# Linear attention in a hybrid decoder step: the output formed with tokens on partitions

## Chip, cores and metric

The kernel runs on one core of one Trainium2 chip. The metric is the device time of one execution in microseconds (us), lower is better. Engines are called as in the profile: PE (TensorE, matmuls), PEld (its weight loads), DVE (VectorE), ACT (ScalarE), POOL (GpSimd) and SP (the engine that issues most DMAs). In a matmul one operand is *stationary* (loaded into the array) and the other is *moving* (streamed through it); all tensors here are float32, and each float32 matmul shows as two records in the trace.

## What is computed

One layer of a decoder trunk for 512 prompt tokens and 8 single-token samples, width 1024. The layer has a modulated layer norm, one large projection, a recurrent branch A, a gated linear attention branch B, a merge of both, and a mixture of experts. The change touches branch B only:

```python
# per head h of 4 (dk=128, dv=256), in chunks of 64 tokens; S: state of 128x256
attn  = where(tri, q_in @ k_in.T, 0)             # 64x64 per chunk and head
o     = attn @ v + q_in @ S_start                # 64x256 per chunk and head
S     = S * decay + k_out.T @ v
# samples, one token each, with a state of their own:
S_s   = S_s * exp(la) + outer(k, v);   o_s = q @ S_s
# both:
o     = o * rsqrt(mean(o**2) + 1e-6) * gla_norm_g   # mean over the 256 values of a head
y_b   = o * silu(gate)
```

## The kernel before, in words

Activations lie with features on the 128 partitions and the 520 tokens (512 + 8) along the free dimension: `hT`, `G` (the gate after silu), `O` (branch B's output), `Q` (q and k), `A` and `Z` are all 8 x 520 per partition. The kernel is written with explicit semaphores, one instruction stream for each engine. PE's work is a fixed list of jobs (`plan_jobs`, L81): job number n writes PSUM banks 2*(n%3) and the next one, so there is a ring of three slots; `start` (L1459) waits until the job three earlier was freed by its reader, `done` counts a job, and other engines wait for that count (`await_job`). Bank 6 holds scores, bank 7 the attention output.

Weights come as 2 MB tiles through a ring; SP issues each load (L466) once PE has reported an older tile as used. Column tiles of `w_in`, `p_a` and `p_b` are used by `project` (L1486), 16 matmuls of 128x128 by 260 columns for one job (helper line L1482).

The stage in question is the chunk loop (PE L1610, DVE L1167, ACT L910), 8 chunks and at the same time 8 samples. For chunk n PE does in this order:

1. scores of 4 heads, 64 columns each (L1616), into bank 6;
2. the state's increment `ds`, 4 matmuls of 256 columns (L1621);
3. half 0 of the gate projection `gg` (L1628, helper L1482);
4. the output, features on partitions: for each of 8 (head, half) pairs one matmul with the values stationary and the masked scores moving (L1636, 64 columns) and, from chunk 1 on, one with the state stationary and q moving (L1639);
5. half 1 of `gg` (L1641), then a wait for DVE's sample state (L1644);
6. the sample's output `os`: 8 matmuls with its state stationary and one moving column (L1647).

DVE masks the scores (L1176, L1178), updates `S` from `ds` (L1187, L1189), decays the sample's state (L1196) and adds the outer product (L1199), then reports `st_ready`. SP then loads the next sample's values broadcast to all partitions (L507), stores the finished state (L514) and loads the one after the next (L494). ACT applies silu to `gg` (L906), copies `os` (L913) and the output out of bank 7 into `O` (L916).

After the loop the norm is made for all tokens at once, beside the projection `ga`: ACT squares a head (L922), PE sums over the features with a matmul of ones (`squares`, L1656, job `ss`, 4 matmuls of 260 columns for one of 4 heads), DVE scales (L1205), ACT takes the root (L926), DVE the reciprocal (L1211) and two multiplies (L1213), then the gating (L1217). Then follow `pa`, `ga`, `pa`, `gb`, `pb`, `gb`, `pb` in groups of four jobs, the output projection `wo`, routing and the experts.

ACT keeps one table of functions; a change of function set shows as ACT_TABLE_LOAD.

Of the kernel before, what the change touches and what calls it, by code (L numbers as in the profile page):

```python
# [27 lines left out]
P = 128  # L28
D = 1024
# [51 lines left out]
def plan_jobs():  # L81
# [21 lines left out]
    for n in range(NCH):  # L103
        jobs += [("ds", n), ("gg", n), ("os", n)]
    for c in range(4):
        jobs += [("ga", c), ("ss", c)]
    jobs += [("pa", c) for c in range(4)]
# [43 lines left out]
def build(nc, t, outs):  # L151
# [6 lines left out]
    with ExitStack() as ctx:  # L158
# [49 lines left out]
        attm = [area(TB + 2048 + 256 * j, HEADS, CH) for j in range(2)]  # L208
        sq = [area(TB + 1040 * j, 2, NT) for j in range(2)]
        rms = [area(TB + 2080 + NT * j, NT) for j in range(2)]  # L210
        bc = area(A0, 4, D)
# [52 lines left out]
        scan_mask = area(2 * WT + 3080, NT)  # L264
        v_samp = area(2 * WT, D)
        v_samp = keep(D)

        rt = [TB]
# [109 lines left out]
        st_out = [sem(f"st_out{j}") for j in range(2)]  # L378
        sq_ready = sem("sq_ready")
        var_ready = sem("var_ready")  # L380
        rms_ready = sem("rms_ready")
        mod_out = sem("mod_out")
        mod_back = sem("mod_back")
# [225 lines left out]
        def _(pool):  # L609
# [34 lines left out]
            link(pool.memset(scan_mask[:, 0:T:CH], 0.0))  # L644
            link(pool.memset(scan_mask[:, T:NT], 0.0))
            pool.sem_inc(consts, 1)

# [95 lines left out]
        def _(sc):  # L743
# [160 lines left out]
            def gate(c):  # L904
                await_job(sc, ("gg", c))
                sc.activation(halves(G[:, c, :]), two_halves(("gg", c)), ACT.Silu, bias=fp[:, c, R_BIN + 4:R_BIN + 5])\  # L906
                  .then_inc(freed(("gg", c)), 1)

            sc.wait_ge(mod_out, 16)
            for n in range(NCH):  # L910
                gate(n)
                await_job(sc, ("os", n))
                sc.activation(O[:, :, T + n:T + n + 1], slot_banks(("os", n))[:, 0, 0:8].unsqueeze(2), ACT.Copy)\  # L913
                  .then_inc(freed(("os", n)), 1)
                sc.wait_ge(o_done, n + 1)
                sc.activation(O[:, :, n * CH:(n + 1) * CH], ps[:, 7, :].rearrange("p (a b) -> p a b", b=CH), ACT.Copy)\  # L916
                  .then_inc(o_copied, 1)

            def square(h):
                if h >= 2:  # L920
                    await_job(sc, ("ss", h - 2))
                sc.activation(sq[h % 2], O[:, 2 * h:2 * h + 2, :], ACT.Square).then_inc(sq_ready, 1)  # L922

            def root(h):
                sc.wait_ge(var_ready, h + 1)
                sc.activation(rms[h % 2], rms[h % 2], ACT.Sqrt).then_inc(rms_ready, 1)  # L926

# [7 lines left out]

            sc.wait_ge(o_copied, NCH)
            sc.wait_ge(freed(("os", 7)), INDEX[("os", 7)] // 3 + 1)
            for j in range(2):
                sc.wait_ge(st_out[j], 16 * (NS // 2))
            square(0)  # L940
            sc.wait_ge(s_out, 32)
            merge_gate("ga", 0)
            square(1)
            for h in range(3):
                root(h)
                merge_gate("ga", h + 1)
                if h < 2:
                    square(h + 2)
            root(3)
            for c in range(4, 8):  # L950
                merge_gate("ga", c)
# [78 lines left out]
        def _(v):  # L1030
# [116 lines left out]
            def copy_vt(c):  # L1147
# [16 lines left out]
            for c in range(2, 8):  # L1164
                copy_vt(c)

            for n in range(NCH):  # L1167
                q = 64 * (n % 2)
# [3 lines left out]
                if n == 0:  # L1172
                    v.wait_ge(kt_ready, 1)

                am = attm[n % 2][q:q + 64]
# [27 lines left out]
            def variance(h):  # L1203
                await_job(v, ("ss", h))
                link(v.tensor_scalar(halves(rms[h % 2]), two_halves(("ss", h)), 1.0 / DVH, RMS_EPS, ALU.mult, ALU.add))  # L1205
                v.sem_inc(freed(("ss", h)), 1)
                v.sem_inc(var_ready, 1)

            def rescale(h):
                v.wait_ge(rms_ready, h + 1)  # L1210
                link(v.reciprocal(rms[h % 2][:], rms[h % 2][:]))  # L1211
                for d in range(2):
                    link(v.scalar_tensor_tensor(O[:, 2 * h + d, :], O[:, 2 * h + d, :], fp[:, 4 + d, R_MISC:R_MISC + 1],  # L1213
                                                rms[h % 2][:], ALU.mult, ALU.mult))

            def gate(c):
# [3 lines left out]
            v.wait_ge(freed(("gg", 7)), INDEX[("gg", 7)] // 3 + 1)  # L1220
            variance(0)
            variance(1)
            for h in range(HEADS):
                rescale(h)
                if h + 2 < HEADS:
                    variance(h + 2)
                gate(2 * h)
                gate(2 * h + 1)

# [228 lines left out]
        def _(pe):  # L1458
# [149 lines left out]
            pe.wait_ge(kt_ready, 1)  # L1608

            for n in range(NCH):  # L1610
                q, tile = 64 * (n % 2), n // 2
# [39 lines left out]
            def squares(h):  # L1651
                pe.wait_ge(sq_ready, h + 1)
                out = start(("ss", h))
                for half in range(2):
                    for d in range(2):
                        ins = pe.matmul(out[:, half, 0:HALF], ones[:], sq[h % 2][:, d, half * HALF:(half + 1) * HALF],  # L1656
                                        start=(d == 0), stop=(d == 1))
# [189 lines left out]
```

## Time and profile before

| | us |
|---|---|
| median of 3 runs | 1518.23 |
| lowest, highest run | 1515.2, 1527.52 |
| span of the profiled execution | 1523.0 |
| PE busy in it | 1262.4 |
| DVE, ACT, POOL busy | 413.6, 307.3, 127.0 |

The span of the profiled execution is the only time given of it; the three other runs were not profiled. Times in the trace count from the span's start. `PEclk` is the mean clock that the chip granted TensorE, as a share of the full 2.4 GHz; it has two levels, 1.2 and 2.4 GHz, so a mean of 0.75 is half the stretch at either. "[0.68 <-DVEq L1201]" means: the engine was idle for 0.68 us before this instruction and what ended that was DVE's queue at line 1201. "x16" counts records, two for a float32 matmul.

### The profile page before, as it was taken

To read this page: it belongs to the slowest core of one execution; us is meant where nothing else is said; L and a number is where in the kernel's file an instruction comes from. 1 tells how busy PE (TensorE), PEld (TensorE's weight loads), DVE (VectorE), ACT (ScalarE), POOL (GpSimd) and SP (SyncE) were. 2 spreads that over 40 slices of the span, in tenths; PEclk is the share of its full clock that TensorE was granted. 3 is DMA by queue.
4 is the path that set the end of the run, shared out by engine and by line. 5 is a ranking of instruction groups with operands and counts; after the bars stand their busy time and mean duration, and the time that the engine had idled before them with its cause. 6 is when DMAs were issued, how large, how long until landed. Compare 5 with 4: busy or idle time off the path is not lost.

```text
span 1523.0 us, 18481 instructions
## 1 busy us (share of the span) xinstructions
PE 1262.4 (83%) x6402; PEld 815.4 (54%) x6403; DVE 413.6 (27%) x704; ACT 307.3 (20%) x433; POOL 127.0 (8%) x203
## 2 busy tenths in 40 slices
PE   3899999999999999999987379798887977788710
PEld 3687878787878888888643223233332332233300
DVE  3326240423332260010386601111111111111156
ACT  3255550410000320000100012121211111111221
POOL 0100000000000000000000111111111111111134
PEclk9899999998878999999998579999998999889965
DMA  8744412124232213413003457996999999999631
GB/s 286 238 171 157 176 56 69 48 72 151 83 110 70 84 56 114 165 56 111 31 15 155 193 194 299 389 348 262 396 397 379 393 367 394 383 378 391 259 119 55
DMA packets 69930, 307.24 MB, mean 202 GB/s; under 512 B 10039, under 2 KB 18744, under 8 KB 56917
## 3 DMA queue, kind: packets, MB, share of 16 engines
q1 hardware_dynamic: 59786, 294.77, 50.5%
q0 software_dynamic: 6272, 10.14, 2.1%
q10 hardware_dynamic: 3820, 1.60, 0.4%
q8 instruction: 38, 0.62, 0.2%
q14 instruction: 14, 0.11, 0.0%
HBM read 298.35 MB, written 18.55 MB: 208 GB/s over the span
## 4 chain that ended last, share of the span: by engine, by line
PE 64%; DMA 18%; DVE 8%; issue 4%; ACT 3%; SPq 2%; ACTq 0%; POOL 0%; POOLq 0%; DVEq 0%; PEldq 0%
PE ps L1482 33%; DMA mem<-in_we_up 13%; PE ps L1750 12%; PE ps L1759 5%; PE ps L1709 3%; DMA mem<-in_w_mod 2%; PE ps L1639 2%; PE ps L1742 2%; PE ps L1636 1%; PE ps L1621 1%; DVE mem L1445 1%; PE ps L1647 1%; DMA mem<-in_we_gate 1%; DVE mem L1444 1%; PE ps L1515 1%
## 5 line engine op out<-in xcount | busy, mean ns | idle before, releaser
L1482 PE MATMUL ps<-mem 128*128 128x260 f32 (+1 forms) x2336 | 546.6, 396 | 10.3 <-ACT mem L813 3.9
L1482 PEld LDWEIGHTS ps<-mem 128*128 128x128 f32 (+1 forms) x2336 | 454.5, 196 | 95.3 <-issue 12.6
L1750 PE MATMUL ps<-mem 128*64 128x512 f32 x1120 | 286.7, 671 | 99.9 <-DMA mem<-in_we_up 78.4
L1750 PEld LDWEIGHTS ps<-mem 128*64 128x64 f32 x1120 | 89.7, 154 | 270.9 <-issue 270.9
L1424 DVE TENSOR_TENSOR mem<-mem,ps 64x512 f32<-64x512 f32 x35 | 24.1, 690 | 431.3 <-ACT mem L1002 431.3
L1759 PE MATMUL ps<-mem 128*64 128x512 f32 x560 | 129.2, 604 | 3.4 <-issue 3.4
L1002 ACT ACT_TABLE_LOAD x35 | 44.9, 1283 | 372.5 <-PE ps L1750 372.5
L1759 PEld LDWEIGHTS ps<-mem 128*64 128x64 f32 x560 | 37.5, 138 | 66.8 <-issue 64.5
L710 POOL DMA_INDIRECT pair_scratch<-mem x35 | 32.7, 934 | 458.2 <-DVE mem L1416 458.2
L1416 DVE COPY mem<-ps 64x512 f32<-64x512 f32 x70 | 48.1, 688 | 78.1 <-PE ps L1759 77.0
L1709 PE MATMUL ps<-mem 128*128 128x512 f32 x128 | 59.8, 628 | 0.0
L1742 PEld LDWEIGHTS ps<-mem 64*128 64x128 f32 x288 | 34.4, 200 | 32.6 <-issue 32.6
L931 ACT ACTIVATE mem<-ps,mem 128x520 f32<-128x520 f32 x16 | 11.1, 694 | 169.9 <-PE ps L1482 169.8
L1742 PE MATMUL ps<-mem 64*128 64x64 f32 x288 | 39.4, 278 | 4.0 <-DMA mem<-hf_scratch,mem 4.0
L651 POOL IOTA mem<- 128x4 int32 x1 | 0.1, 137 | 510.0 <-DVEq L1218 510.0
L1709 PEld LDWEIGHTS ps<-mem 128*128 128x128 f32 x128 | 25.4, 201 | 31.7 <-issue 31.6
L688 POOL DMA_INDIRECT mem<-hf_scratch,mem x37 | 35.9, 970 | 31.5 <-POOL mem L719 29.7
L1814 PEld LDWEIGHTS ps<-mem 64*128 64x128 f32 x140 | 19.4, 210 | 29.5 <-issue 29.5
L1238 DVE TENSOR_TENSOR mem<-mem,ps 128x520 f32<-128x520 f32 x8 | 5.6, 696 | 102.9 <-PE ps L1482 102.9
L906 ACT ACTIVATE mem<-ps,mem 128x520 f32<-128x520 f32 x8 | 5.6, 694 | 133.8 <-PE ps L1482 133.8
L1009 ACT ACTIVATE mem<-ps 128x256 f32<-128x256 f32 x35 | 13.5, 384 | 94.0 <-PE ps L1814 94.0
L1515 PE MATMUL ps<-mem 128*9 128x128 f32 x768 | 25.9, 292 | 5.2 <-DMA mem<-in_w_mod 5.2
(284 smaller groups left out, 988.7 us busy)
## 6 DMA issues: line engine op xcount, KB each, us to landing
mem<-in_we_gate SPq DMA_DIRECT2D x32, 2048.0 KB, 12.0
mem<-in_we_up SPq DMA_DIRECT2D x32, 2048.0 KB, 16.5
mem<-in_we_down SPq DMA_DIRECT2D x32, 2048.0 KB, 8.9
mem<-in_w_in SPq DMA_DIRECT2D x14, 2048.0 KB, 8.5
mem<-in_w_mod SPq DMA_DIRECT2D x12, 2048.0 KB, 12.0
out<-mem SPq DMA_DIRECT2D x13, 512.0 KB, 5.3
mem<-in_state_gla SPq DMA_DIRECT2D x8, 512.0 KB, 3.9
mem<-v_scratch SPq DMA_DIRECT2D x8, 512.0 KB, 4.3
```

Source lines behind the costliest of these rows:

```text
L688: pool.indirect_dma_start(xg[j][0:CAP, :], None, hf_dram, bass.IndirectOffsetOnAxis(ap=gidx[j][0:CAP, 0:1], axis=0), bounds_check=NT - 1, ...
L710: pool.indirect_dma_start(pair_dram, bass.IndirectOffsetOnAxis(ap=sidx[j][0:CAP, 0:1], axis=0), yb[j][0:CAP, :], None, bounds_check=PAIRS ...
L1002: sc.activation(sg[j][CAP:2 * CAP, :], ps[0:CAP, 2 + j, :], ACT.Silu).then_inc(sg_ready[j], 1)
L1416: v.tensor_copy(yb[j][0:CAP, q * 512:(q + 1) * 512], ps[CAP * q:CAP * q + CAP, 4 + j, :])\
L1424: v.tensor_tensor(act[j][0:CAP, :], sg[j][CAP:2 * CAP, :], ps[CAP:2 * CAP, 2 + j, :], ALU.mult)\
L1482: ins = pe.matmul(out[0:m, h, 0:HALF], w[:, k, col:col + m], src[:, k, h * HALF:(h + 1) * HALF], start=(k == 0), stop=(k == KD - 1))
L1515: pe.matmul(o, cs[:, k, :], w[:, k, g * P:(g + 1) * P], start=(k == 0), stop=False)
L1639: ins = pe.matmul(o, S[n % 2][:, h, d * P:(d + 1) * P], Q[:, h, cols], start=False, stop=True)
L1709: ins = pe.matmul(out[0:r, h, :], Z[:, k, i * P:i * P + r], wo[h][:, k, :], start=(k == 0), stop=(k == KD - 1))
L1742: ins = pe.transpose(ps[:, j, k * CAP:(k + 1) * CAP], xg[j][0:CAP, :].rearrange("s (p k) -> s k p", k=KD)[:, k, :], ident[0:CAP, 0:CAP])
L1750: ins = pe.matmul(ps[CAP * q:CAP * q + CAP, 2 + j, :], xT[j][:, k, :], ring[3 * slot + q][:, k, :], start=(k == 0), stop=(k == KD - 1))
L1759: ins = pe.matmul(ps[CAP * q:CAP * q + CAP, 4 + j, :], acT[j][:, k, :], wd[:, k, q * 512:(q + 1) * 512], start=(k == 0), stop=(k == 3))
```

## The change

Step 4 is turned round. The masked scores of a head are now stationary (64 columns) and that head's 256 values move; for the second term q is stationary and the state moves. Two heads lie side by side: head 2a writes PSUM partitions 0 to 63, head 2a+1 partitions 64 to 127. The scores tile is padded with zero rows to 128. The output now has tokens on partitions, so the mean over a head's features is along the free dimension, and ACT forms it for each chunk (square with a running sum, root, with DVE's reciprocal between, two scaled copies into `osb`). Four PE transposes of 128x128 for each chunk, put into the `os` job of the next chunk, turn it back, and ACT writes them into `O`. The sample's output is formed with a masked q stationary (32 columns for each head, four heads side by side) and the state moving; DVE sums it over samples, and it is normed once. The `ss` jobs, the long norm and their buffers are gone; two small jobs, `oT` and `sT`, take the last transposes.

```diff
-    for c in range(4):
-        jobs += [("ga", c), ("ss", c)]
+    jobs += [("ga", 0), ("oT", 0), ("ga", 1), ("sT", 0), ("ga", 2), ("ga", 3)]
...
+            link(pool.memset(qm[:], 0.0))
+            link(pool.affine_select(out=qm[:], in_=qm[:], compare_op=ALU.not_equal, fill=1.0, base=0,
+                                    pattern=[[0, HEADS], [1, NS], [-1, 32]], channel_multiplier=0))
...
+            def mean_squares(o, junk, k):
+                link(sc.activation(junk, o, ACT.Square, scale=DVH ** -0.5, accum_out=o_ms[:, k // 2, k % 2:k % 2 + 1]))
+            def heads_of(n):
+                sc.wait_ge(o_done, n + 1)
...
+                for a in range(2):
+                    mean_squares(o[:, a, :], osb[n % 2][:, a, :], 2 * n + a)
+                sc.activation(o_rs[:, n, :], o_ms[:, n, :], ACT.Sqrt, bias=rms_eps[:, 0:1]).then_inc(root_ready, 1)
+                sc.wait_ge(rms_ready, n + 1)
+                for a in range(2):
+                    ins = sc.activation(osb[n % 2][:, a, :], o[:, a, :], ACT.Copy, scale=o_rs[:, n, a:a + 1])
...
+            def fill_heads(n, src):
+                for d in range(2):
+                    for hh in range(2):
...
+                        ins = sc.activation(dst, src[:, (2 * hh + d) * P:(2 * hh + d + 1) * P].rearrange("p (a i) -> p a i", a=2),
+                                            ACT.Copy, scale=fp[:, 4 + d, R_MISC:R_MISC + 1])
...
             for n in range(NCH):
+                heads_of(n)
                 gate(n)
                 await_job(sc, ("os", n))
-                sc.activation(O[:, :, T + n:T + n + 1], slot_banks(("os", n))[:, 0, 0:8].unsqueeze(2), ACT.Copy)\
-                  .then_inc(freed(("os", n)), 1)
-                sc.wait_ge(o_done, n + 1)
-                sc.activation(O[:, :, n * CH:(n + 1) * CH], ps[:, 7, :].rearrange("p (a b) -> p a b", b=CH), ACT.Copy)\
-                  .then_inc(o_copied, 1)
...
+                if n >= 1:
+                    fill_heads(n - 1, slot_banks(("os", n))[:, 1, :]).then_inc(freed(("os", n)), 1)
...
+            link(v.tensor_tensor(qm[:], qm[:], qs.unsqueeze(3).to_broadcast([P, HEADS, NS, 32]), ALU.mult))
...
+            def gather_samples(n):
+                await_job(v, ("os", n))
+                src = slot_banks(("os", n))[:, 0, 0:DVH]
+                link(v.tensor_copy(os_sum, src) if n == 0 else v.tensor_tensor(os_sum, os_sum, src, ALU.add))
...
                 v.sem_inc(attm_ready, 1)
+                if n >= 1:
+                    gather_samples(n - 1)
                 await_job(v, ("ds", n))
...
                 v.sem_inc(st_ready, 1)
+                inverse_root(n)
...
+            def transpose_heads(out, n):
+                pe.wait_ge(o_copied, n + 1)
+                for k in range(4):
+                    ins = pe.transpose(out[:, 1, k * P:(k + 1) * P], osb[n % 2][:, k // 2, (k % 2) * P:(k % 2 + 1) * P], ident[:])
...
-                for hd in range(8):
-                    h, d = hd // 2, hd % 2
-                    o = ps[:, 7, hd * CH:(hd + 1) * CH]
-                    ins = pe.matmul(o, v_tok[q:q + 64, tile, hd * P:(hd + 1) * P], attm[n % 2][q:q + 64, h, :],
-                                    start=True, stop=(n == 0))
-                    if n:
-                        ins = pe.matmul(o, S[n % 2][:, h, d * P:(d + 1) * P], Q[:, h, cols], start=False, stop=True)
+                for a in range(2):
+                    for b in range(2):
+                        h = 2 * a + b
+                        ins = pe.matmul(ps[64 * b:64 * b + 64, 7, a * DVH:(a + 1) * DVH], attm[n % 2][:, h, :],
+                                        v_tok[:, tile, h * DVH:(h + 1) * DVH], start=True, stop=(n == 0))
+                    for b in range(2 if n else 0):
+                        h = 2 * a + b
+                        ins = pe.matmul(ps[64 * b:64 * b + 64, 7, a * DVH:(a + 1) * DVH], Q[:, h, cols], S[n % 2][:, h, :],
+                                        start=False, stop=True)
...
                 pe.wait_ge(st_ready, n + 1)
+                if n >= 1:
+                    pe.wait_ge(os_summed, n)
                 out = start(("os", n))
-                for hd in range(8):
-                    ins = pe.matmul(out[:, 0, hd:hd + 1], st[n % 2][:, hd // 2, (hd % 2) * P:(hd % 2 + 1) * P],
-                                    qs[:, hd // 2, n:n + 1], start=True, stop=True)
-                done(ins)
+                for h in range(HEADS):
+                    ins = pe.matmul(out[32 * h:32 * h + 32, 0, 0:DVH], qm[:, h, n, :], st[n % 2][:, h, :], start=True, stop=True)
+                if n >= 1:
+                    ins = transpose_heads(out, n - 1)
+                done(ins)
...
-                        if a == "ga" and c < 4:
-                            squares(c)
+                        if (a, c) == ("ga", 0):
+                            done(transpose_heads(start(("oT", 0)), NCH - 1))
+                            pe.wait_ge(os_summed, NS)
+                        if (a, c) == ("ga", 1):
+                            pe.wait_ge(osb_ready, 1)
+                            out = start(("sT", 0))
+                            for d in range(2):
+                                ins = pe.transpose(out[:, 0, d * P:(d + 1) * P], osb[0][:, 0, d * P:(d + 1) * P], ident[:])
+                            done(ins)
```

## Rows read from the trace of the kernel before

**Rows 1.** The page: busy times, and the granted clock in 40 slices

```profile
PE 1262.4 (83%) x6402; PEld 815.4 (54%) x6403; DVE 413.6 (27%) x704; ACT 307.3 (20%) x433; POOL 127.0 (8%) x203
...
PEclk9899999998878999999998579999998999889965
```

**Rows 2.** Stretches: before the loop, chunks 0 to 2, the `ss` stage; columns as headed

```profile
core 0: us, PE busy (x) PEld busy (x) DVE busy (x) ACT busy (x) POOL busy (x), PEclk, DMA share, GB/s
339.40:343.90 4.50, 3.56 (x26) 2.71 (x27) 1.94 (x4) 2.29 (x5) 0.00 (x0) 1.00 0.73 247
343.90:358.40 14.50, 13.80 (x81) 11.61 (x81) 5.88 (x14) 2.48 (x4) 0.00 (x0) 1.00 0.58 194
358.40:382.30 23.90, 23.90 (x98) 19.04 (x97) 6.12 (x14) 1.36 (x3) 0.00 (x0) 0.71 0.34 102
382.30:402.80 20.50, 20.50 (x98) 16.85 (x97) 6.11 (x14) 1.36 (x3) 0.00 (x0) 0.83 0.27 78
...
509.50:544.70 35.20, 35.20 (x162) 30.54 (x162) 13.35 (x11) 19.29 (x21) 0.00 (x0) 1.00 0.17 59
```

**Rows 3.** Waits in the loop, 343.9 to 509.5: total us, times, longest

```profile
ACT mem L906 <- PE ps L1482: 133.8, 7, 21.6
...
PE ps L1647 <- DVEq L1201: 0.7, 1, 0.7
PE ps L1647 <- PE ps L1482: 0.6, 2, 0.3
```

**Rows 4.** Timeline of PE, chunk 0: start, us, engine, line, records, idle before

```profile
343.92 0.65 PE L1616 MATMUL ps<-mem 128*64 128x64 f32 x8 [0.20 <-ACTq L902]
344.50 1.99 PE L1621 MATMUL ps<-mem 64*128 64x256 f32 x8
346.42 3.77 PE L1482 MATMUL ps<-mem 128*128 128x260 f32 x16
350.12 2.00 PE L1636 MATMUL ps<-mem 64*128 64x64 f32 x16
352.05 3.77 PE L1482 MATMUL ps<-mem 128*128 128x260 f32 x16
...
356.50 1.95 PE L1647 MATMUL ps<-mem 128*128 128x1 f32 x16 [0.68 <-DVEq L1201]
```

**Rows 5.** Timeline of chunk 2, PE and SP

```profile
382.25 0.68 PE L1616 MATMUL ps<-mem 128*64 128x64 f32 x8
...
388.49 0.29 PEld L1636 LDWEIGHTS ps<-mem 64*128 64x128 f32 x2 [0.34 <-issue]
...
390.86 0.33 SPq L507 DMA_DIRECT2D mem<-v_scratch  x1
...
392.85 0.43 PE L1636 MATMUL ps<-mem 64*128 64x64 f32 x2
393.21 0.69 PE L1639 MATMUL ps<-mem 128*128 128x64 f32 x2
393.83 0.69 PE L1636 MATMUL ps<-mem 64*128 64x64 f32 x2
...
394.93 6.25 PE L1482 MATMUL ps<-mem 128*128 128x260 f32 x16
```

**Rows 6.** The chain of waits, first `ss` job after the loop: start, us

```profile
516.82 1.75 PE ps L1656 x8
```

**Rows 7.** Timelines: transposes; four column groups; two column groups

```profile
342.62 1.09 PE L1605 MATMUL ps<-mem 128*128 128x128 f32 x8 [0.59 <-DVEq L1152]
...
746.48 3.64 PE L1704 MATMUL ps<-mem 128*8 128x256 f32 x64
...
1119.67 3.65 PE L1759 MATMUL ps<-mem 128*64 128x512 f32 x16
```

**Rows 8.** Groups of ACT: busy us, mean ns, idle before

```profile
L1009 ACT ACTIVATE mem<-ps 128x256 f32<-128x256 f32 x35 | 13.5, 384 | 94.0 <-PE ps L1814 94.0
L931 ACT ACT_TABLE_LOAD x5 | 6.4, 1283 | 5.5 <-PE ps L1482 5.4
L906 ACT ACTIVATE mem<-ps,mem 128x520 f32<-128x520 f32 x8 | 5.6, 694 | 133.8 <-PE ps L1482 133.8
```

**Rows 9.** DMA issues in 355 to 510: count, KB, median us to landing

```profile
out<-mem SPq DMA_DIRECT2D x9, 512.0 KB, 5.3
mem<-v_scratch SPq DMA_DIRECT2D x7, 512.0 KB, 4.4
```

More of the change, by code:

```diff
@@ L208, in build @@
         attm = [area(TB + 2048 + 256 * j, HEADS, CH) for j in range(2)]
-        sq = [area(TB + 1040 * j, 2, NT) for j in range(2)]
-        rms = [area(TB + 2080 + NT * j, NT) for j in range(2)]
         bc = area(A0, 4, D)
@@ L264, in build @@
         scan_mask = area(2 * WT + 3080, NT)
-        v_samp = area(2 * WT, D)
         v_samp = keep(D)
+        qm = keep(HEADS, NS, 32)
+        osb = [keep(2, DVH), v_samp[:, 256:768].rearrange("p (a b) -> p a b", b=DVH)]
+        os_sum = v_samp[:, 0:256]
+        o_ms = keep(NCH + 1, 2)
+        o_rs = keep(NCH + 1, 2)
+        rms_eps = keep(1)
         rt = [TB]
@@ L378, in build @@
         st_out = [sem(f"st_out{j}") for j in range(2)]
-        sq_ready = sem("sq_ready")
-        var_ready = sem("var_ready")
+        root_ready = sem("root_ready")
         rms_ready = sem("rms_ready")
+        osb_ready = sem("osb_ready")
+        os_summed = sem("os_summed")
+        O_filled = sem("O_filled")
         mod_out = sem("mod_out")
@@ L907, in gate @@
                   .then_inc(freed(("gg", c)), 1)
+            def mean_squares(o, junk, k):
+                link(sc.activation(junk, o, ACT.Square, scale=DVH ** -0.5, accum_out=o_ms[:, k // 2, k % 2:k % 2 + 1]))
+            def heads_of(n):
+                sc.wait_ge(o_done, n + 1)
+                if n >= 2:
+                    await_job(sc, ("os", n - 1))
+                if n == 1:
+                    sc.wait_ge(vs_out, 16)
+                o = ps[:, 7, :].rearrange("p (a b) -> p a b", b=DVH)
+                for a in range(2):
[4 more added lines that the diff above has]
+                    ins = sc.activation(osb[n % 2][:, a, :], o[:, a, :], ACT.Copy, scale=o_rs[:, n, a:a + 1])
+                    if a == 0:
+                        link(ins)
+                    else:
+                        ins.then_inc(o_copied, 1)
@@ new lines, in fill_heads @@
+            def fill_heads(n, src):
+                for d in range(2):
+                    for hh in range(2):
+                        dst = O[:, 4 * hh + d:4 * hh + d + 3:2, n * CH:(n + 1) * CH]
+                        ins = sc.activation(dst, src[:, (2 * hh + d) * P:(2 * hh + d + 1) * P].rearrange("p (a i) -> p a i", a=2),
+                                            ACT.Copy, scale=fp[:, 4 + d, R_MISC:R_MISC + 1])
+                        if d + hh < 2:
+                            link(ins)
+                return ins
@@ L919, in square @@
[L919 to L926, printed above, removed]
+                if n >= 1:
+                    fill_heads(n - 1, slot_banks(("os", n))[:, 1, :]).then_inc(freed(("os", n)), 1)
+                else:
+                    sc.sem_inc(freed(("os", n)), 1)
@@ new lines, in _ @@
+            sc.wait_ge(os_summed, NS)
+            mean_squares(os_sum, osb[0][:, 0, :], 2 * NCH)
+            sc.activation(o_rs[:, NCH, 0:1], o_ms[:, NCH, 0:1], ACT.Sqrt, bias=rms_eps[:, 0:1]).then_inc(root_ready, 1)
+            sc.wait_ge(rms_ready, NCH + 1)
+            sc.activation(osb[0][:, 0, :], os_sum, ACT.Copy, scale=o_rs[:, NCH, 0:1]).then_inc(osb_ready, 1)
+            await_job(sc, ("oT", 0))
+            fill_heads(NCH - 1, slot_banks(("oT", 0))[:, 1, :]).then_inc(freed(("oT", 0)), 1)
@@ L928, in merge_gate, with fill_samples @@
+            def fill_samples():
+                await_job(sc, ("sT", 0))
+                for d in range(2):
+                    src = slot_banks(("sT", 0))[:, 0, d * P:(d + 1) * P].rearrange("p (h r) -> p h r", r=32)[:, :, 0:NS]
+                    link(sc.activation(O[:, d::2, T:NT], src, ACT.Copy, scale=fp[:, 4 + d, R_MISC:R_MISC + 1]))
+                sc.sem_inc(freed(("sT", 0)), 1)
+                sc.sem_inc(O_filled, 1)
             def merge_gate(job, c):
@@ L934, in merge_gate @@
                 sc.sem_inc(sig_ready, 1)
-            sc.wait_ge(o_copied, NCH)
-            sc.wait_ge(freed(("os", 7)), INDEX[("os", 7)] // 3 + 1)
             for j in range(2):
                 sc.wait_ge(st_out[j], 16 * (NS // 2))
-            square(0)
             sc.wait_ge(s_out, 32)
             merge_gate("ga", 0)
[L943 to L950, printed above, removed]
+            fill_samples()
+            for c in range(1, 8):
                 merge_gate("ga", c)
@@ L1165, in _, with inverse_root @@
                 copy_vt(c)
+            def gather_samples(n):
+                await_job(v, ("os", n))
+                src = slot_banks(("os", n))[:, 0, 0:DVH]
+                link(v.tensor_copy(os_sum, src) if n == 0 else v.tensor_tensor(os_sum, os_sum, src, ALU.add))
+                v.sem_inc(os_summed, 1)
+            def inverse_root(n):
+                v.wait_ge(root_ready, n + 1)
+                v.reciprocal(o_rs[:, n, :] if n < NCH else o_rs[:, n, 0:1],
+                             o_rs[:, n, :] if n < NCH else o_rs[:, n, 0:1]).then_inc(rms_ready, 1)
             for n in range(NCH):
@@ L1173, in _ @@
                     v.wait_ge(kt_ready, 1)
+                    for k in range(2):
+                        link(v.memset(attm[k][64 - 64 * k:P - 64 * k], 0.0))
                 am = attm[n % 2][q:q + 64]
@@ L1201, in _ @@
                 v.sem_inc(st_ready, 1)
[L1203 to L1216, printed above, removed]
+                inverse_root(n)
+            gather_samples(NS - 1)
+            inverse_root(NCH)
+            v.wait_ge(O_filled, 1)
+            v.wait_ge(freed(("gg", 7)), INDEX[("gg", 7)] // 3 + 1)
+            for c in range(KD):
                 link(v.tensor_tensor(O[:, c, :], O[:, c, :], G[:, c, :], ALU.mult))
                 v.sem_inc(yb_ready, 1)
[L1220 to L1228, printed above, removed]
             for c in range(KD):
@@ L1608, in _ @@
             pe.wait_ge(kt_ready, 1)
+            def transpose_heads(out, n):
+                pe.wait_ge(o_copied, n + 1)
+                for k in range(4):
+                    ins = pe.transpose(out[:, 1, k * P:(k + 1) * P], osb[n % 2][:, k // 2, (k % 2) * P:(k % 2 + 1) * P], ident[:])
+                return ins
             for n in range(NCH):
@@ L1644, in _ @@
                 pe.wait_ge(st_ready, n + 1)
+                if n >= 1:
+                    pe.wait_ge(os_summed, n)
                 out = start(("os", n))
-                for hd in range(8):
-                    ins = pe.matmul(out[:, 0, hd:hd + 1], st[n % 2][:, hd // 2, (hd % 2) * P:(hd % 2 + 1) * P],
-                                    qs[:, hd // 2, n:n + 1], start=True, stop=True)
-                done(ins)
[L1651 to L1657, printed above, removed]
+                for h in range(HEADS):
+                    ins = pe.matmul(out[32 * h:32 * h + 32, 0, 0:DVH], qm[:, h, n, :], st[n % 2][:, h, :], start=True, stop=True)
+                if n >= 1:
+                    ins = transpose_heads(out, n - 1)
                 done(ins)
@@ L1664, in _ @@
                         project((a, c), w, (c % 4) * P, P, hT)
-                        if a == "ga" and c < 4:
-                            squares(c)
+                        if (a, c) == ("ga", 0):
[4 more added lines that the diff above has]
+                            out = start(("sT", 0))
+                            for d in range(2):
+                                ins = pe.transpose(out[:, 0, d * P:(d + 1) * P], osb[0][:, 0, d * P:(d + 1) * P], ident[:])
+                            done(ins)
                     last_of_tile((a, 4 * g + 3))
```

2 lines of the change are left out of this document (added).

## The prediction

> **What bounds the kernel now.** I read the page first. PE is busy for 83% of the span and no other engine for more than 27%, and the granted clock dips in the slices from about 340 to 500 us [rows 1]. So I cut that stretch, the chunk loop, at the starts of its chunks and read the windows. Chunk 0 is 14.5 us long at full clock; the next are 23.9 and 20.5 us long, and PE is busy for every microsecond of them, but at a mean clock of 0.71 and 0.83 [rows 2]. The seven chunks after the first are of these two kinds: two like the former, five like the latter (20.4 to 21.0 us). The view of waits agrees: in the whole loop PE waited 0.7 us for DVE and 0.6 us otherwise, while ACT waited 134 us for PE's gate projection [rows 3]. PE alone sets this stage, twice over: by the number of its instructions and by the clock it is granted. The loop lasts from 343.9 to 509.5 us, 165.6 us. After it, in the `ss` stage, PE is busy for all of 35.2 us at full clock [rows 2], so whatever leaves PE there is gained too. From there to the output projection PE runs back to back on jobs that the change doesn't touch, so a gain made in the loop carries to the end.
>
> **What a chunk costs PE at full clock.** From starts in chunk 0: scores 0.58, `ds` 1.92, first gate half 3.70, second about 3.77 [rows 4]; sum 9.97 us, untouched by the change. The old output of a later chunk is 16 matmuls at 0.363 us (0.36 from one start to the next, 392.85 to 393.21 [rows 5]), 5.8 us, and the old `os` 1.7 to 1.9 us [rows 4]. That makes 17.5 us at full clock; the 3 us above it in a 20.5 us chunk are clock. A mean of 0.83 over 20.5 us is 7 us at the low level, which costs 3.5 us; 0.71 over 23.9 us is 14 us, costing 7 us. Over seven chunks: 2 x 7 + 5 x 3.5 = 31 us. What PE did before the fall: in chunk 2 it was inside the output matmuls, whose spacing goes from 0.36 to 0.62 at 393.2 us [rows 5], after 4.7 us of them; the following gate half starts slow and takes 6.1 us instead of 3.77.
>
> **What the change does to PE.**
> - *Output.* 8 matmuls of 256 columns, 16 records, two heads in two column halves. The nearest row is the experts' down projection, also 64 stationary columns in two halves: 16 records of 512 columns in 3.65 us [rows 7], 0.228 a record; at 256 columns 0.114, so 16 take 1.8 us, with the tail 1.9. Lower bound: that. Upper bound: no overlap of the halves. A dense 260-column record is 3.77/16 = 0.23 us [rows 4], so 16 x 0.23 = 3.7 us. I take 1.9, because the nearest row has the same shape.
> - *os.* 4 matmuls in four column groups, 8 records. The output projection of the samples does the same with 256 columns: 64 records in 3.64 us, 0.057 each [rows 7], so 0.46; without overlap 8 x 0.23 = 1.8. I take 0.5.
> - *Transposes.* 8 took 1.09 us [rows 7]; 4 make 0.5 us.
> - *Changes of shape.* Before the 64-row output matmuls PE's weight load stood 0.34 us idle for "issue" [rows 5]; that one is inside the 3.70 above. Two new changes (gate to `os`, `os` to transposes) cost between 0 and 0.68 us; I take 0.3.
>
> The Trainium skill (TensorEngine Tiling (Array Packing), Key Properties) says that a change of tiling mode drains the engine. The trace agrees in kind: alternating 64-row and 128-row matmuls are spaced at 0.36 us [rows 5], and 64-row ones alone in chunk 0 at 1.93/8 = 0.24 [rows 4]. At 0.12 us for each of four new changes a chunk would cost 0.5 instead of the 0.3 that I add, 1.4 us over the loop.
>
> New chunk: 9.97 + 1.9 + 0.5 + 0.5 + 0.3 = 13.2 us; seven of them 92.4 us. Chunk 0 is set by something else: PE waited there for DVE's sample state until 356.50 [rows 4], which came through the values' trip to memory and back. That stays, so the shorter output only lengthens PE's idle time from 0.7 to 1.7 us; then 0.5 for `os`: 13.1 us. Loop: 105.5 us at full clock, 60.1 less.
>
> After the loop four `ss` jobs of 1.75 us go [rows 6], 7.0 us; `oT` (0.5) and `sT` (0.3) come: 6.2 us less. Together 66.3 us.
>
> **The clock.** The fall in chunk 2 came inside the old output matmuls [rows 5], which go, so I expect these dips to go with them. One dip I leave in: chunk 1, which comes after a wait of 0.7 us and the one-column matmuls [rows 4], has twice the low time of chunk 2 [rows 2], and that wait gets longer. Its price is 3.4 us. Bounds: none (0) and one for each chunk (8 x 3.4 = 27). Net 62.9 us.
>
> **What lies beside PE, and what it hides under.** ACT's chunk grows from 1.4 us busy [rows 2] to this chain from the end of the output: two squares of 256 at 0.38 plus a sum of unknown price (0 to 0.4 each; I take 0.1), a table load 1.28, a root 0.2, DVE's reciprocal 0.2 with its signals, two copies at 0.38, a table load 1.28, silu 0.69 [rows 8], about 5.9 us with the handoffs. Silu frees the slot which the next gate half needs: PE comes there 3.77 + 0.5 + 0.5 + 0.3 + 0.58 + 1.92 = 7.6 us after the output's end. Cover 1.7 us; without it each chunk would pay the rest. The four copies into `O` (1.5 us) follow and end long before the next output. Behind ACT's new wait for the reciprocal stand silu and these copies, and for them PE's slots. DVE's new wait for the root sits behind `st_ready`, so SP's DMAs don't wait for it; behind it stands the next chunk's masking, needed 4.4 us later at the earliest. DVE itself has the sample state ready 8.6 us after the scores' start (SP's load at 390.86 against 382.25 [rows 5]), 9.1 with the new sum; PE asks for it after 11.9 us. The DMA turn for one sample (values landing in 4.4 us, store in 5.3 [rows 9]) fits: values issued at 9.1 land at 13.5, DVE wants them about 20 us after that scores' start. DVE's masked q (about 1.1 us) and POOL's fill come ahead of the loop, where the value projection's dense PE work covers them; uncovered 1 us. The long norm on DVE and ACT beside `ga` had nothing on the path, so its going is worth nothing.
>
> **Sum.** Profiled span 1523.0 - 62.9 = 1460.1 us. The median of the runs lies 4.8 below that span, inside their own spread of 12 us; I take the same step off the median: 1518.2 - 62.9 = 1455.3, say 1455 us.
>
> **Rivals.**
> 1. *The clock goes on dipping once a chunk.* For it: the scores, transposes and four-group matmuls make about 2 us of short work between the gate halves. Against it: the transposes ahead of the loop ran at clock 1.00 with idle time in between [rows 2]. Seven dips more, 24 us: 1479. The Trainium skill (TensorE: Matmul & The Clock Gate, Part 4: PE-mode transpose) says that transposes don't count as busy in the same way for the clock; the same rows, 4.5 us of transposes at 1.00, don't bear that out. By that rule this rival would be the likeliest.
> 2. *ACT's chain becomes the bound.* If the sums or handoffs cost 3 us more, each chunk waits 1.3 to 3 us in front of a gate half: 9 to 21 us, about 1470. For it: the cover is only 1.7 us. Against it: ACT's rows are short and regular.
> 3. *The heads don't run side by side.* Output 3.7 and `os` 1.8: 3.1 us more a chunk, 22 us: 1477. Against it: both rows of [rows 7].
> 4. *The other side: the clock stays at its low level through the whole loop.* Then about 105 us become up to 210, 45 more than now, less 6 after the loop: 1557. It decides from about three quarters of the loop at the low level (13.2 us x 1.65 is above today's 21). Against it: PE, with sparser work, is low today in some 40% of the loop.
>
> **How the numbers follow.** Chances: forecast 0.66 (own range 1446 to 1464: no dip and no cost for shapes, or 0.7 for these and one more dip), rival 1 0.15, rival 2 0.11, rival 3 0.05, rival 4 0.02, 0.01 for the rest. The range takes in all of the forecast's and of rival 2, and most of rivals 1 and 3: 1444 to 1482. A measurement of this kernel tells about 1% (15 us) from no change; all cases but rival 4 gain more: faster 0.96, same 0.02, slower 0.02.
>
> **What would show it.** Right: chunks of 13 to 13.5 us, windows of the loop at clock near 1, output of 1.9 and `os` of 0.5 us, the `ga` stage free of other PE work but 0.8 us. Wrong: PE idle in front of a gate half on ACT (rival 2), records of 0.2 us in the output (rival 3), windows at 0.8 (rival 1); or a gain in the loop that DMA waits among the experts take back.

## The result

The changed kernel takes 1448.07 us (median of 4 runs, 1443.2 to 1451.11) against 1519.68 us before: a ratio of 0.9523, 95% interval 0.9489 to 0.9556, some 72 us less. The forecast, 1455 us of 1518.2, is a ratio of 0.958: the right direction, some 8 us short. The profiled execution has a span of 1449.3 us (its own time is 1.8 us above that), 73.7 less than the one before.

Its page, busy times and granted clock, against [rows 1]:

```profile
PE 1193.1 (82%) x6220; PEld 751.4 (52%) x6221; DVE 398.4 (27%) x708; ACT 335.5 (23%) x511; POOL 129.1 (9%) x206
...
PEclk9899999999999999999995699999999989999955
```

A slice is some 36 us. The dip of the loop, slices 10 to 13 before, is gone; what is left, at slices 22 and 23 (the end of routing and the start of the experts; 22 to 24 before) and at the span's end, was there before. The windows cut at the starts of the chunks (the columns are those of [rows 2]) show chunks 0, 1, 2, 3 and 7, then the projections that took the place of the `ss` stage:

```profile
342.70:356.80 14.10, 11.60 (x65) 8.54 (x65) 6.60 (x17) 3.40 (x9) 0.00 (x0) 1.00 0.54 186
356.80:373.00 16.20, 16.20 (x80) 11.63 (x76) 6.71 (x16) 6.92 (x13) 0.00 (x0) 0.79 0.55 163
373.00:386.00 13.00, 13.00 (x78) 9.51 (x77) 6.70 (x16) 6.84 (x15) 0.00 (x0) 1.00 0.39 113
386.00:399.40 13.40, 13.01 (x77) 9.53 (x76) 6.71 (x16) 7.23 (x16) 0.00 (x0) 1.00 0.38 124
...
438.30:451.60 13.30, 13.00 (x79) 9.62 (x77) 6.71 (x16) 7.14 (x15) 0.00 (x0) 1.00 0.30 93
451.60:480.80 29.20, 28.89 (x137) 24.74 (x135) 6.19 (x10) 10.30 (x22) 3.70 (x22) 1.00 0.19 72
```

A chunk takes 13.0 to 13.4 us at clock 1.00, where it was 20.4 to 23.9 us; only chunk 1 still has a dip. PE is still busy for nearly all of it. Its waits in the loop, as totals in us, times and longest, are 2.5 us for DVE's sample state in chunk 0 and 0.7 us in front of two later `os` jobs, where the kernel before had 0.6 [rows 3]:

```profile
PE ps L1700 <- DVEq L1261: 2.5, 1, 2.5
PE ps L1700 <- PE ps L1524: 0.7, 2, 0.4
```

The timeline of chunk 2, PE and ACT, its start and then from the end of the first gate half:

```profile
373.02 0.68 PE L1665 MATMUL ps<-mem 128*64 128x64 f32 x8
...
379.26 0.65 PE L1685 MATMUL ps<-mem 128*64 128x256 f32 x4
...
379.74 0.60 PE L1689 MATMUL ps<-mem 128*64 128x256 f32 x4
...
381.13 3.77 PE L1524 MATMUL ps<-mem 128*128 128x260 f32 x16
381.25 0.38 ACT L919 ACTIVATE mem<-ps 128x256 f32<-128x256 f32 x1 [5.70 <-PE ps L1689]
381.53 0.20 ACT L919 ACTIVATION_READ_ACCUMULATOR mem<-ps 128x1 f32 x1
...
382.25 1.28 ACT L931 ACT_TABLE_LOAD   x1
383.55 0.29 ACT L931 ACTIVATE mem<-mem 128x2 f32<-128x2 f32 x1
...
384.07 0.98 ACT L934 ACTIVATE mem<-ps,mem 128x256 f32<-128x256 f32 x2 [0.23 <-DVE mem L1220]
...
384.84 0.64 PE L1700 MATMUL ps<-mem 128*32 128x256 f32 x8
385.07 1.28 ACT L914 ACT_TABLE_LOAD   x1
...
385.41 0.66 PE L1656 MATMUL ps<-mem 128*128 128x128 f32 x4
...
386.00 0.68 PE L1665 MATMUL ps<-mem 128*64 128x64 f32 x8
386.37 0.69 ACT L914 ACTIVATE mem<-ps,mem 128x520 f32<-128x520 f32 x1
...
388.52 3.77 PE L1524 MATMUL ps<-mem 128*128 128x260 f32 x16
```

Read it by starts. The output lasts from 379.26 to 381.13, 1.87 us for 16 records (0.117 each); `os` from 384.84 to 385.41, 0.57; the transposes to 386.00, 0.59; the next gate half starts at 388.52. ACT's chain from the output's end (381.13) to the end of silu (387.06) is 5.9 us, and PE wants that slot 1.5 us later.

To see where the time went, the spans of all profiled executions are cut at the same five places: the loop's first score matmul, the first projection behind the loop, the first transpose of the recurrent branch's outputs (the end of the projections), the experts' first and last matmul group. The table is worked out from the starts in the timelines; the loop's clock is from its window. A kernel for which no median is given below ran once. The experts' stage ends here with the last matmul; the first expectation below counts it to the start of the last group, 4 to 5 us earlier (568.2 and 559.8 us there are 572.6 and 564.6 here).

```
kernel          span    ahead  loop   proj.  route  experts rest  loop's clock
before          1523.0  343.9  165.7  235.0  135.8  572.6   70.0  0.81
before_again    1519.9  344.1  166.0  235.1  135.9  568.9   69.9  0.81
before_shift4   1515.1  343.6  161.8  235.1  135.7  568.9   70.0  0.83
padded_old      1481.5  342.0  130.5  235.1  135.3  568.6   70.0  0.92
after           1449.3  342.7  108.9  229.2  133.9  564.6   70.0  0.97
after_again     1447.8  343.9  105.4  229.2  134.4  564.9   70.0  1.00
early_values    1440.2  342.0  103.0  229.2  134.4  561.7   69.9  1.00
heads_apart     1453.7  343.0  115.1  229.2  134.4  562.2   69.8  0.97
transposes_x4   1458.7  341.9  119.7  230.5  134.5  561.9   70.2  0.96
act_extra1      1453.6  342.0  110.1  229.2  134.2  568.3   69.8  0.95
act_extra3      1456.2  343.3  114.7  229.2  134.7  564.3   70.0  0.97
after_shift1    1448.6  342.7  108.7  229.2  133.8  564.2   70.0  0.97
after_shift4    1455.2  344.8  109.1  229.1  134.2  568.1   69.9  0.97
```

Between the first profiles the loop lost 56.8 us, the projections 5.8, together 62.6 us; the forecast had 62.9 for them. The other 11 us came from elsewhere: 8.0 in the experts' stage and 1.9 in routing, which the edit doesn't touch, and 1.2 ahead of the loop, a stretch that scatters from 341.9 to 344.8 us over all the profiles. The experiments on the experts' stage look into the largest of these.

### The profile page after: what moved, and what is told of

It reads as the page before. It is cut to its first block, busy times and chain, and to the rows that moved or that the text cites. A ratio compares the mean times of both kernels' runs of the same rounds, so it can differ in the third digit from the quotient of the medians.

```text
span 1449.3 us, 18209 instructions
## 1 busy us (share of the span) xinstructions
PE 1193.1 (82%) x6220; PEld 751.4 (52%) x6221; DVE 398.4 (27%) x708; ACT 335.5 (23%) x511; POOL 129.1 (9%) x206
## 4 chain that ended last, share of the span: by engine, by line
PE 63%; DMA 18%; DVE 9%; issue 4%; ACT 3%; SPq 2%; ACTq 0%; POOL 0%; POOLq 0%; DVEq 0%; PEldq 0%
PE ps L1524 33%; DMA mem<-in_we_up 14%; PE ps L1802 13%; PE ps L1811 6%; PE ps L1761 3%; PE ps L1794 2%; DMA mem<-in_w_mod 2%; PE ps L1670 1%; DVE mem L1487 1%; PE ps L1557 1%; DMA mem<-in_we_gate 1%; DVE mem L1486 1%; PE ps L1743 1%; PE ps L1685 0%; DVE mem L1485 0%
## 5 line engine op out<-in xcount | busy, mean ns | idle before, releaser
L1524 PE MATMUL ps<-mem 128*128 128x260 f32 (+1 forms) x2336 | 528.1, 386 | 10.8 <-ACT mem L821 3.9
L1524 PEld LDWEIGHTS ps<-mem 128*128 128x128 f32 (+1 forms) x2336 | 440.8, 190 | 93.2 <-issue 16.1
L982 ACT ACTIVATE mem<-ps,mem 128x520 f32<-128x520 f32 x16 | 11.1, 693 | 175.3 <-PE ps L1524 175.1
L1051 ACT ACTIVATE mem<-ps 128x256 f32<-128x256 f32 x35 | 13.4, 383 | 94.0 <-PE ps L1866 94.0
L1280 DVE TENSOR_TENSOR mem<-mem,ps 128x520 f32<-128x520 f32 x8 | 5.6, 696 | 102.9 <-PE ps L1524 102.9
L1275 DVE TENSOR_TENSOR mem<-mem,ps 128x520 f32<-128x520 f32 x8 | 5.6, 697 | 87.7 <-PE ps L1524 87.7
```

Of the source, the lines that this page charges most:

```text
L1524: ins = pe.matmul(out[0:m, h, 0:HALF], w[:, k, col:col + m], src[:, k, h * HALF:(h + 1) * HALF], start=(k == 0), stop=(k == KD - 1))
```

## The experiments

**The same kernel again.** 

> The changed kernel once more, for the stages that its edit does not touch. In the first profile the loop lost 56.8 us and the ss stage 5.9 us, as the forecast had it, and another 8.3 us went from the experts' stage (568.2 us in the kernel before, 559.8 us in the changed one). Theory: the 8.3 us is scatter of the experts' weight loads from one execution to the next; then this execution's experts' stage lies anywhere between about 555 and 570 us, and its loop at 109 us. Rival: the earlier start gains something there for good; then the experts' stage is 560 us again within 2 us.

Measured: 1447.6 us, ratio 0.9529 (0.9507 to 0.9551). Experts' stage 564.9 us against 564.6: the rival, as far as one repeat goes. Later kernels that differ from it by one and by four small matmuls gave 564.2 and 568.1, so a scatter of some 4 us is there too. The loop took 105.4 us, and this time chunk 1 had no dip: the clock over the whole loop was 1.00. So the dip behind chunk 0's wait comes in some executions and not in others.

**Do the two heads have to be neighbours?**

```diff
-                for a in range(2):
-                    for b in range(2):
-                        h = 2 * a + b
...
+                for b in range(2):
+                    for a in range(2):
+                        h = 2 * a + b
...
```

> Same matmuls, other order: the output of the two heads in one column half first, then that of the two in the other half, so that no two neighbours use different halves. Theory (two neighbours in different halves stream at the same time): 16 records at about 0.21 to 0.23 us in series, 3.4 to 3.7 us instead of 1.9 for a chunk, +1.6 us x 7 chunks = +11 us, about 1459 us. Rival (the gain comes from longer moving operands alone, the halves don't overlap or overlap in any order): the output stays at 1.9 us, no change.

Measured: 1451.8 us, ratio 0.9563 (0.9546 to 0.958). The timeline of PE in chunk 2 of this kernel:

```profile
380.35 0.65 PE L1685 MATMUL ps<-mem 128*64 128x256 f32 x2
380.83 0.59 PE L1688 MATMUL ps<-mem 128*64 128x256 f32 x2
381.27 0.65 PE L1685 MATMUL ps<-mem 128*64 128x256 f32 x4
381.70 0.65 PE L1688 MATMUL ps<-mem 128*64 128x256 f32 x4
382.19 0.59 PE L1685 MATMUL ps<-mem 128*64 128x256 f32 x2
382.62 0.59 PE L1688 MATMUL ps<-mem 128*64 128x256 f32 x2
383.14 3.77 PE L1524 MATMUL ps<-mem 128*128 128x260 f32 x16
```

The output takes 2.79 us. Where a row has two records, two fit into 0.43 to 0.48 us: that is one stream at a time. Where it has four, four fit into the same time: there the second head of one half and the first of the other ran together, though the program has them one behind the other. So half of the overlap was lost, not all of it: the theory holds for neighbours in one half, but PE also overlapped matmuls across the boundary. 0.92 us x 7 chunks is 6.4 us, and the loop is 6.2 us longer than in the first profile, which has the same dip in chunk 1.

**The old form without the change of rows.** The old output's first matmul contracts over 64 rows, its second over 128. This edit of the kernel before pads the former to 128, with zero rows as the changed kernel has them:

```diff
+                    for k in range(2):
+                        link(v.memset(attm[k][64 - 64 * k:P - 64 * k], 0.0))
...
-                    ins = pe.matmul(o, v_tok[q:q + 64, tile, hd * P:(hd + 1) * P], attm[n % 2][q:q + 64, h, :],
+                    ins = pe.matmul(o, v_tok[:, tile, hd * P:(hd + 1) * P], attm[n % 2][:, h, :],
```

> The kernel before with one edit: its values-times-scores matmul reads all 128 rows (scores padded with zero rows), so the output's matmuls no longer alternate between 64 and 128 rows. Theory (the alternation costs about 0.12 us for each matmul): spacing 0.36 falls to 0.24 us, output 5.8 to 3.9 us for a chunk at full clock, 7 x 1.9 = 13 us less, and up to 10 us more if the clock dips shrink with it: 1497 to 1507 us. Rival (the spacing is set by weight loads of 128 columns for 64 moving ones): no change.

Measured: 1485.39 us, ratio 0.9795 (0.9775 to 0.9815): 32 us, more than expected, from one matmul with longer operands and a fill with zeros. PE's timeline in chunk 1 and the window of the whole loop:

```profile
364.52 0.39 PE L1641 MATMUL ps<-mem 128*128 128x64 f32 x2
364.74 0.39 PE L1638 MATMUL ps<-mem 128*128 128x64 f32 x2
364.97 0.39 PE L1641 MATMUL ps<-mem 128*128 128x64 f32 x2
```
```profile
342.00:472.50 130.50, 128.76 (x753) 112.08 (x753) 49.25 (x114) 11.99 (x25) 0.00 (x0) 0.92 0.40 127
```

The spacing is 0.22 us, where it was 0.36 [rows 5]: 16 x 0.14 x 7 = 16 us. The rest is clock. Before, a loop of 165.7 us at 0.81 is 63 us at the low level; here 130.5 us at 0.92 is 21 us. 42 us less at half rate is worth 21 us, and 16 + 21 = 37 is what the loop lost (35.2) within 2 us. The profiled execution was the fastest of its four; by the medians the gain is 32 us. The Trainium skill (TensorEngine Tiling (Array Packing), Key Properties) says that a change of tiling mode drains the engine; the trace agrees, at 0.14 us for each such change, and shows that the alternation also went with low clock. Nearly half of the gain of the whole change is thus to be had without turning anything round.

**Chunk 0's wait.**

```diff
+            sp.wait_ge(vt_ready, 8)
+            sp.dma_start(vs_dram, v_samp[0:NS, :]).then_inc(vs_out, 16)
             load_state(0)
             load_state(1)
-            sp.wait_ge(vt_ready, 8)
-            sp.dma_start(vs_dram, v_samp[0:NS, :]).then_inc(vs_out, 16)
             sp.wait_ge(vs_out, 16)
```

> The changed kernel with one move in SP's queue: the samples' values are stored to memory ahead of the first two state loads, not behind them, so that they come back some 3 us earlier. Theory (PE's 2.5 us wait at the end of chunk 0 is that trip, and the low clock in chunk 1 follows from the wait): the wait goes, chunk 1 falls from 16.2 to 13.0 us, together 5 to 6 us less, about 1442 us. Rival (the low clock in chunk 1 has another cause): 2.5 us less and chunk 1 still 16 us long.

Measured: 1444.06 us, ratio 0.9523 (0.95 to 0.9547), 3.5 us below the changed kernel's median on the same chip; the intervals overlap, so the total alone doesn't settle it. The timeline does. First the changed kernel, then this one, at the end of chunk 0:

```profile
349.94 3.77 PE L1524 MATMUL ps<-mem 128*128 128x260 f32 x16
356.19 0.64 PE L1700 MATMUL ps<-mem 128*32 128x256 f32 x8 [2.48 <-DVEq L1261]
```
```profile
349.17 3.77 PE L1524 MATMUL ps<-mem 128*128 128x260 f32 x16
352.88 0.64 PE L1700 MATMUL ps<-mem 128*32 128x256 f32 x8
```

The wait is gone, the loop takes 103.0 us at clock 1.00, 2.4 less than the repeat without a dip. As to the dip: of the nine profiles of the new form eight have this wait, and seven of the eight have a loop clock of 0.95 to 0.97; the one without the wait has none. That fits the theory, but one profile without the dip also has the wait, so a single profile of this kernel doesn't prove it.

**The kernel before again.** 

> The kernel before once more, for its experts' stage. From the first experts' matmul to the last it took 572.6 us in the first profile; the changed kernel and three others took 564.6, 564.9, 562.2 and 561.7, the padded old form 568.6. Theory (scatter of the weight loads): anywhere from 562 to 573 us. Rival (the change shortens this stage): 570 us or more. The loop should be 160 to 170 us again, at a clock near 0.81.

Measured: span 1519.9 us, experts' stage 568.9 us, loop 166.0 us at 0.81. The stage lies inside the theory's band and just under the rival's; but see the table: over all runs it is 568.6 to 572.6 us in four profiles of the old form and 561.7 to 568.3 in nine of the new, with means of 569.8 and 564.5. The bands come within 0.3 us of each other, every profile of the old form lies above every one of the new, and the means differ by 5 us: more than scatter, so the theory alone doesn't hold.

**Transposes and the clock.**

```diff
-                for k in range(4):
+                for k in [i % 4 for i in range(16)]:
                     ins = pe.transpose(out[:, 1, k * P:(k + 1) * P], osb...
```

> The changed kernel with each chunk's four transposes done four times over (same output). Theory (transposes hold the clock like other matmuls): 12 x 0.12 = 1.45 us more for each of seven chunks, loop 10 us longer (115 to 119 us), its clock still 0.97 to 1.0. Rival (the Trainium skill, TensorE: Matmul & The Clock Gate, Part 4: PE-mode transpose: transposes don't count as busy in the same way for the clock): the clock falls once a chunk, loop clock 0.8 to 0.9, loop 125 to 145 us.

Measured: span 1458.7 us. The 16 transposes of chunk 2 of this kernel, then the windows of the dip in chunk 1 and of the stretch behind it:

```profile
387.67 1.97 PE L1656 MATMUL ps<-mem 128*128 128x128 f32 x16
```
```profile
356.00:374.00 18.00, 18.00 (x82) 13.09 (x79) 6.71 (x16) 7.08 (x13) 0.00 (x0) 0.72 0.51 147
374.00:388.50 14.50, 14.50 (x93) 11.04 (x92) 6.69 (x16) 7.15 (x15) 0.00 (x0) 1.00 0.30 104
```

The loop is 10.8 us longer than in the first profile. A chunk at full clock takes 14.28 us from score to score, 1.31 more than the 12.97 there: 9.2 us for seven chunks. The rest is a longer dip in chunk 1, which ends ahead of that chunk's transposes. The loop's clock of 0.96 over 119.7 us is 9.6 us at the low level, and the 18 us at 0.72 hold all of that (10.1). Two microseconds of transposes in each chunk don't bring the low clock here. So this trace doesn't bear out the rule of the Trainium skill that the expectation cites (TensorE: Matmul & The Clock Gate, Part 4: PE-mode transpose); longer stretches of transposes were not tried.

**ACT's cover.** Copies of the output's halves, written over by the squares that follow, lengthen ACT's chain; EXTRA stands for the 1 or 3 of the two runs:

```diff
                 for a in range(2):
+                    for again in range(EXTRA):
+                        link(sc.activation(osb[n % 2][:, a, :], o[:, a, :], ACT.Copy))
                     mean_squares(o[:, a, :], osb[n % 2][:, a, :], 2 * n + a)
```

With EXTRA = 1: 

> The changed kernel with one more copy of each half on ACT ahead of the squares of each chunk, about 1.0 us more in ACT's chain (its output is written over). In the trace silu frees the slot 1.4 us before the next gate half wants it. Theory (that cover): no change, loop 103 to 109 us. Rival (ACT's chain is already on the path): loop 7 us longer.

With EXTRA = 3: 

> The same with three more copies of each half, about 3.0 us. Theory (cover 1.4 us, then each microsecond counts in each of seven chunks): 1.6 x 7 = 11 us, loop 115 to 120 us, and PE idle in front of the gate half for ACT. Rival (ACT is nowhere near the path): loop 103 to 109 us.

Measured: with one, PE has no wait for ACT in the loop (its length, 110.1 us, has a dip like the first profile's 108.9). With three, the loop is 114.7 us long, 5.8 us more than in the first profile and half of the 11 expected; the view of PE's waits in it, and chunk 2:

```profile
PE ps L1526 <- ACT mem L914: 5.8, 6, 1.0
```
```profile
390.95 3.77 PE L1526 MATMUL ps<-mem 128*128 128x260 f32 x16 [1.01 <-ACT mem L914]
```

The three copies took 2.5 us, not 3, and PE waited 1.0 us a chunk, in six chunks: the cover is 1.5 us, as the timeline said, and what exceeded it was paid by PE.

**Why the experts' stage differs.** In front of the first matmuls of each of the experts' 35 groups PE has idle time; part of it is put down to the weights' DMA, part to nothing that the profile shows ("issue"). The timelines of the third group in the kernel before and in the changed one:

```profile
912.46 1.51 PE L1750 MATMUL ps<-mem 128*64 128x512 f32 x6 [1.41 <-issue]
```
```profile
845.78 1.51 PE L1802 MATMUL ps<-mem 128*64 128x512 f32 x6 [1.21 <-issue]
```

The group after it has 1.20 and 0.90. The code there is the same, and the gaps repeat to 0.02 us or so in the unedited repeats. Three kernels move PE's later instructions along by repeating the first matmul of the `plan` job (same output):

```diff
-            for k in range(5):
+            for k in [0] * N + list(range(5)):
```

> The changed kernel with one extra matmul of one stationary column (a repeat of the first one of the plan job, same output) just ahead of the experts' loop, so that every later instruction of PE stands a little further on in its stream; it costs 0.1 us itself. In front of the experts' first matmuls PE waited for nothing shown ('issue') 20.0 to 20.2 us in the three programs of the old form and 14.5 to 16.8 us in seven of the new form, 4.5 us, with the same code there. Theory (where PE's instructions lie sets how long its sequencer takes in the loop): the sum moves, to 18 us or more or to 13 or less. Rival (it depends on something else that the change altered): 14.5 to 16.8 again.

> The same with four extra matmuls. Theory (the place in the stream): the sum of 'issue' moves out of 14.5 to 16.8 us here or with one extra matmul. Rival: it stays in both.

> The kernel before with four extra matmuls at the same place. Theory (the place in the stream): the sum moves away from 20.0 to 20.2 us, by 1 us or more. Rival: 20 us again. The whole experts' stage takes 562 to 573 us in any case, as its weight loads scatter.

Measured: the sums of this "issue" time are 14.6, 15.6 and 18.5 us. In the changed kernel nothing moved; in the kernel before it did, by 1.5 us, and the gap of that fourth group fell from 1.20 to 1.02:

```profile
921.24 7.09 PE L1750 MATMUL ps<-mem 128*64 128x512 f32 x32 [1.02 <-issue]
```

So the gaps aren't fixed by the loop's own code, and moving the instructions can change them; but it didn't in two of three, and the theory isn't shown. Nor is the sum a measure of the same gaps in all kernels. The view counts 12 or 13 gaps as "issue" in the old form and 9 to 11 in the new, where later ones are put down to the weights' DMA. The groups of the kernel before, the changed one, and the one before with four extra matmuls:

```profile
L1750 PE MATMUL ps<-mem 128*64 128x512 f32 x1120 | 286.7, 671 | 99.9 <-DMA mem<-in_we_up 78.4 <-issue 20.0 <-DMA mem<-in_we_gate 1.5
L1802 PE MATMUL ps<-mem 128*64 128x512 f32 x1120 | 284.9, 667 | 93.4 <-DMA mem<-in_we_up 76.6 <-issue 15.5 <-DMA mem<-in_we_gate 1.3
L1750 PE MATMUL ps<-mem 128*64 128x512 f32 x1120 | 285.1, 668 | 97.6 <-DMA mem<-in_we_up 77.9 <-issue 18.5 <-DMA mem<-in_we_gate 1.3
```

Nine gaps, in front of groups 1 to 5 and 10 to 13, are "issue" in every kernel. They add up to 16.0 to 16.2 us in the three unmoved kernels of the old form, 14.5 to 14.8 in the nine of the new, and 14.8 in the kernel before with four extra matmuls. So they are worth 1.5 us and not 5. And in that last kernel, with gaps as short as in the changed one, the experts' stage took 568.9 us, as long as in the plain repeat. The shorter gaps therefore don't explain the 5 us by which the stage is shorter on average, and the cause of those stays open.

## Why the prediction was right

- *What bounds the stage.* Right: PE alone, by its instructions and by its clock. Once the loop had begun, PE's only waits were 2.5 us for chunk 0's values and 0.7 us for two later `os` jobs.
- *A chunk's sum.* Forecast 13.2 us, measured 12.98 from score to score (373.02 to 386.00). Output 1.87 for 1.9, `os` 0.57 for 0.5, transposes 0.59 for 0.5. The 0.3 us for changes of shape isn't there as a term of its own: the weight loads do show gaps of 0.34 to 0.4 us, but these are inside the measured starts; `os` and transposes together came out 0.16 us above their two terms. The rows that set the price were well chosen: two and four column groups overlapped fully when neighbours lie in different groups.
- *The clock.* The steps "I expect these dips to go with them" and "One dip I leave in" came out as put: 1.00 in the chunks from 2 on, one dip in chunk 1, which came in most profiles with the wait. Its price was put at 3.4 us; the chunk took 16.26 us, 3.3 more than the others. The reason was too coarse. I put the dips down to the output matmuls as they were; padding their rows alone took two thirds of the low time away (63 to 21 us), so most of it hung on their alternation, or on the 2.2 us that it cost a chunk; the runs don't part these two. What kept the other third low in that kernel isn't shown.
- *Chunk 0.* Forecast a wait of 1.7 us, measured 2.2 to 2.7; small, and it could be had back by one move in SP's queue.
- *ACT.* Chain 5.9 us, forecast 5.9; cover 1.5, forecast 1.7, and the runs with extra copies agree: 0.8 us more on ACT cost nothing, 2.5 us more cost 1.0.
- *The loop as a whole.* Forecast 105.5 + 3.4 = 108.9 us, measured 108.9 in the first profile. That it fits to a tenth is luck: chunk 0 took 0.9 us more than forecast, chunks 1 to 7 together 0.9 less, and with no dip the repeat took 105.4.
- *After the loop.* Forecast 6.2, measured 5.8 us.
- *The step that was short*: "a gain made in the loop carries to the end". It carries, and stages behind it changed as well: the experts' stage is about 5 us shorter on average (8 in the first pair), routing 1 to 2. Nothing in the profile of before showed that, and it is the larger part of the 8 us between forecast and result.
- *The forecast's own range*, 1446 to 1464 us, is wider than the terms named for it: no dip and no cost for shapes give 1455.3 - 3.4 - 2.1 = 1449.8, the other end 1455.3 + 2.8 + 3.4 = 1461.5. The measured 1448.07 lies just below the first.
- *The rivals.* 1: no dip a chunk. 2: ACT is 1.5 us off the path, nearly as the forecast had it. 3: the heads do run side by side. 4: no chunk but the second has low clock.

## What to carry to other kernels

When a stretch of small matmuls is slow, look at the spacing from start to start and at the shapes of neighbours first: here matmuls with alternating row counts cost 0.14 us each and went with low clock, and zero padding alone gave 32 of some 70 us. Turning a product round, so that the long side moves and two narrow outputs lie side by side in alternation, took another 22 us off the loop (130.5 to 108.9) and 6 off the projections, and its price could be read from rows of the same shape elsewhere in the trace. The rest came in stages that the edit doesn't touch, and isn't explained; a gain elsewhere is not to be booked to an edit because it came with it. Where an engine off the path gets a longer chain, work out from whose slot it frees how many microseconds of cover it has; here 1.5.

## What the runs showed that I had not expected

- A sum along an ACTIVATE shows as an instruction of its own, ACTIVATION_READ_ACCUMULATOR, of 0.2 us behind the 0.38 us square.
- Padding one operand with zero rows took the loop's clock from 0.81 to 0.92.
- PE overlapped matmuls of different column halves across a boundary of program order: eight of 16 records in the order by halves ran two at a time.
- The same loop code on PE had idle gaps 0.2 to 0.3 us shorter in front of two groups of experts in one program than in the other, repeatably, and the stage's length didn't follow them.
